# Mixers' output projections: weight units split four ahead of their tile, a list of banks per tile, more tiles begun early

## The reference, cut to what matters

```python
h = h + rmsnorm(mixed, gain)        # layers 1, 2; mixed = mixer(rmsnorm(h)) @ w_out
h = h + rmsnorm(swiglu_ffn(rmsnorm(h)), gain)
x = x + mixed                       # layers 3, 4: no norm behind the mixer
x = x + conv_ffn(rmsnorm(x))
```

## Time and profile before

| | |
|---|---|
| runs (device us) | 2430.51, 2433.38, 2432.56; median 2432.56 |
| the profiled execution | 2432.12 us, of which the span from the first to the last instruction is 2430.3 us |
| mean granted TensorE clock | 0.994 of full speed |
| busy: PE, PEld, DVE, ACT, POOL | 2376.9 (98%), 1941.5 (80%), 1322.0 (54%), 1020.6 (42%), 60.6 us (2%) |
| DMA | 214.12 MB, 88 GB/s over the span |

### The profile page before, as it was taken

How to read it: one execution, slowest core, us unless ns; L and a number is a source line. 1 busy time by engine, 2 the same in 40 slices (tenths; PEclk the granted TensorE clock), 3 DMA queues, 4 the chain that set the end, 5 groups by cost and what they waited for, 6 DMA issues and landing times.

```text
span 2430.3 us, 29906 instructions
## 1 busy us (share of the span) xinstructions
PE 2376.9 (98%) x11072; PEld 1941.5 (80%) x11072; DVE 1322.0 (54%) x1869; ACT 1020.6 (42%) x1630; POOL 60.6 (2%) x96
## 2 busy tenths in 40 slices
PE   8999999999999999999999989999999999999999
PEld 7777788888788877888887768788888877788887
DVE  5665644432537866444325665777533555677731
ACT  5555423222447854322324664444322544444420
POOL 1000000000002200000000000000001000000000
PEclk9999999999999999999999999999999999999999
DMA  4112222332221112223322113222323222222332
GB/s 147 61 60 71 87 95 87 104 119 89 78 96 61 53 55 87 93 95 102 120 90 80 61 36 112 78 95 95 121 95 102 78 70 70 95 96 95 105 107 82
DMA packets 68785, 214.12 MB, mean 88 GB/s; under 512 B 7056, under 2 KB 17808, under 8 KB 68688
## 3 DMA queue, kind: packets, MB, share of 16 engines
q1 hardware_dynamic: 67280, 210.72, 26.2%
q0 software_dynamic: 1408, 2.08, 0.3%
HBM read 210.67 MB, written 2.10 MB: 88 GB/s over the span
## 4 chain that ended last, share of the span: by engine, by line
PE 92%; DVE 4%; ACT 3%; issue 1%; DMA 0%; SPq 0%; ACTq 0%; DVEq 0%
PE bank L257 25%; PE bank L259 24%; PE bank L258 24%; PE bank L319 7%; PE bank L327 5%; PE bank L916 1%; PE bank L907 1%; PE bank L947 1%; PE bank L1290 1%; DVE w_lo L231 0%; ACT w_hi L226 0%; PE bank L1803 0%; PE bank L2221 0%; PE bank L2233 0%; PE bank L1335 0%
## 5 line engine op out<-in xcount | busy, mean ns | idle before, releaser
L257 PE MATMUL bank<-x_hi,w_hi 128*128 128x512 f32 x1792 | 708.6, 395 | 8.6 <-DVE w_lo L231 7.1
L259 PE MATMUL bank<-x_hi,w_lo 128*128 128x512 f32 x1792 | 699.4, 390 | 0.0
L258 PE MATMUL bank<-x_lo,w_hi 128*128 128x512 f32 x1792 | 699.1, 390 | 0.0
L231 DVE TENSOR_TENSOR w_lo<-raw,w_hi 128x1024 fp32r<-128x1024 f32 (+1 forms) x368 | 471.4, 1291 | 258.4 <-ACT w_hi L226 257.6
L226 ACT ACTIVATE w_hi<-raw 128x1024 fp32r<-128x1024 f32 (+1 forms) x368 | 404.1, 1108 | 115.9 <-PE bank L259 68.1
L257 PEld LDWEIGHTS bank<-x_hi,w_hi 128*128 128x128 f32 x1792 | 337.6, 188 | 83.9 <-issue 13.1
L259 PEld LDWEIGHTS bank<-x_hi,w_lo 128*128 128x128 f32 x1792 | 337.3, 188 | 71.5
L258 PEld LDWEIGHTS bank<-x_lo,w_hi 128*128 128x128 f32 x1792 | 337.8, 189 | 69.9 <-issue 1.9
L258 PE MATMUL bank<-up_a_lo,w_hi 128*128 128x512 f32 x704 | 273.9, 389 | 0.0
L257 PE MATMUL bank<-up_a_hi,w_hi 128*128 128x512 f32 x704 | 273.9, 389 | 0.0
L259 PE MATMUL bank<-up_a_hi,w_lo 128*128 128x512 f32 x704 | 273.9, 389 | 0.0
(11 more groups left out here) (355 smaller groups left out, 2675.1 us busy)
## 6 DMA issues: line engine op xcount, KB each, us to landing
raw<-in_w_up SPq DMA_DIRECT2D x176, 512.0 KB, 3.2
raw<-in_w_down SPq DMA_DIRECT2D x64, 704.0 KB, 4.2
raw<-in_w_fox_qk SPq DMA_DIRECT2D x16, 512.0 KB, 3.2
raw<-in_w_hgrn_qf SPq DMA_DIRECT2D x16, 512.0 KB, 3.2
raw<-in_w_fox_v SPq DMA_DIRECT2D x8, 512.0 KB, 4.0
raw<-in_w_fox_out SPq DMA_DIRECT2D x8, 512.0 KB, 3.2
raw<-in_w_hgrn_v SPq DMA_DIRECT2D x8, 512.0 KB, 3.4
raw<-in_w_hgrn_g SPq DMA_DIRECT2D x8, 512.0 KB, 3.2
```

What stands on the lines that cost most here:

```text
L231: nc.vector.tensor_tensor(w_lo[:, slot, 0:size], raw[:, slot % 2, 0:size], w_hi[:, slot, 0:size].bitcast(F32), ALU.subtract).then_inc(sem( ...
L257: nc.tensor.matmul(out, w[0], x[0], start=first, stop=False)
L258: nc.tensor.matmul(out, w[0], x[1], start=False, stop=False)
L259: return nc.tensor.matmul(out, w[1], x[0], start=False, stop=last)
```

## The change: what it does

- `act_out` and `dve_out` split four units ahead instead of two (`fourth_ahead`): at tile i ACT converts unit i+4 and then empties the tile; DVE does its share of tile i first and then splits unit i+4. Behind the last unit come the first three units of the next phase, at tiles 4 to 6.
- So units 2 and 3 must be split inside the mixer. Fox: `convert` and `split` take `fox_out` 2 and 3 in the last pair. Sb: `convert(10)` before and `convert(11)` behind the copies of `sb_fail_b`, and `split(10)`, `split(11)` before `output(3)` on DVE. Gla: unit 3 for p = 4, behind `mix_hi` on ACT and `mix_lo` on DVE. Hgrn had them already.
- Every mixer has a list with one bank for each of the 8 tiles, and `pe_out` waits for the last tile that had the same bank. Fox goes from two banks to four, gla from (0, 1, 3) to (0, 1, 3, 4, 0, 1, 3, 0); hgrn and sb keep theirs.
- Fox makes 6 blocks of tile 1 before `turn(m, 1)` instead of 3, and 7 blocks of tile 2 around `bring(m)`, with a new wait for the copies of `fox_pt_a`, which empty bank 2. Gla makes 6 blocks of tile 3 early.
- In gla, for p = 4 and 5, DVE norms the previous head before it makes the chunk states, not behind them.

```diff
-        def out_early(pe, name, c, ks, ready, banks=(0, 1)):
+        def out_early(pe, name, c, ks, ready, banks):
...
-            out_products(pe, name, c, u_of(name) + c, ks, ready, not done, False, banks[c % len(banks)])
+            out_products(pe, name, c, u_of(name) + c, ks, ready, not done, False, banks[c])
...
-                    if len(banks) > 2:
-                        if i >= len(banks):
-                            pe.wait_ge(sem("y_ready" if s < 4 else "h_ready"), DT * s + i - len(banks) + 1)
-                    elif (s, j, c) > (0, 0, 1):
-                        bank_free(pe, s, i)
+                    if banks[i] in banks[:i]:
+                        before = i - 1 - banks[:i][::-1].index(banks[i])
+                        pe.wait_ge(sem("y_ready" if s < 4 else "h_ready"), DT * s + before + 1)
...
-        def act_out(act, s, name, banks=(0, 1), split=0):
-            def body(j, u, last):
-                for c in range(4):
-                    if 4 * j + c >= split:
-                        ahead(convert_act, act, name, c, u + c, last)
-                    third_ahead(convert_act, act, name, c, last)
-                    tile_act(act, s, 4 * j + c, banks[(4 * j + c) % len(banks)], u + c)
-            unrolled(name, body)
...
+        def fourth_ahead(convert, eng, name, i):
+
+            e = i + 4
+            if e < DT:
+                convert(eng, e % 4, u_of(name) + e, IN_UNIT)
+            elif e < DT + 3 and name in following:
+                convert(eng, e % 4, following[name].first + e - DT, following[name].size)
+
+        def act_out(act, s, name, banks):
+            for i in range(DT):
+                fourth_ahead(convert_act, act, name, i)
+                tile_act(act, s, i, banks[i], u_of(name) + i)
+
+        def dve_out(dve, s, name, banks):
+            for i in range(DT):
+                tile_dve(dve, s, i, banks[i], u_of(name) + i)
+                fourth_ahead(convert_dve, dve, name, i)
...
+        FOX_OUT = (0, 1, 2, 3) * 2
...
-                out_early(pe, "fox_out", 0, list(range(7)), out_ready)
+                part(0, list(range(7)))
                 turn(m, 0)
-                out_early(pe, "fox_out", 1, list(range(3)), out_ready)
+                part(1, list(range(6)))
                 turn(m, 1)
-                out_early(pe, "fox_out", 1, [3, 4], out_ready)
+                part(1, [6])
+                wait(pe, "fx_pt", 6 * m + 3)
+                part(2, list(range(3)))
                 bring(m)
-                out_early(pe, "fox_out", 1, [5, 6], out_ready)
-            pe_out(pe, 0, "fox_out", out_ready)
+                part(2, list(range(3, 7)))
+            pe_out(pe, 0, "fox_out", out_ready, FOX_OUT)
...
-                elif i < 2 * FOX_PAIRS + 2:
+                elif i < 2 * FOX_PAIRS + 4:
                     convert_act(act, i % 4, u_of("fox_out") + i - 2 * FOX_PAIRS, IN_UNIT)
...
-        HGRN_OUT = (0, 1, 2, 3)
+        HGRN_OUT = (0, 1, 2, 3) * 2
...
+        SB_OUT = (0, 1) * 4
...
             turned(3, 0)
+            convert(10)
             turned(3, 1)
+            convert(11)
             output(3)
             exp_ln_table()
...
             pool_low(3)
+            split(10)
+            split(11)
             output(3)
...
-        GLA_OUT = (0, 1, 3)
+        GLA_OUT = (0, 1, 3, 4, 0, 1, 3, 0)
...
             part(2, [4, 5])
+            part(3, [0, 1, 2, 3, 4, 5])
             pe_out(pe, 6, "gla_out", out_ready, GLA_OUT)
...
+                if mix and not proj:
+                    ahead(convert_act, act, "gla_out", 1, u_out + 1, False)
...
+                if norm and not proj:
+                    normed()
                 if mix:
                     wait(dve, "gla_dec", m + 1)
...
+                if norm and proj:
+                    normed()
...
+                if mix and not proj:
+                    ahead(convert_dve, dve, "gla_out", 1, u_out + 1, False)
```

More of the change, by code:

```diff
@@ L771, in out_products, with pe_out @@
             return ins
-        def out_early(pe, name, c, ks, ready, banks=(0, 1)):
+        def out_early(pe, name, c, ks, ready, banks):
             done = early.setdefault((name, c), [])
-            out_products(pe, name, c, u_of(name) + c, ks, ready, not done, False, banks[c % len(banks)])
+            out_products(pe, name, c, u_of(name) + c, ks, ready, not done, False, banks[c])
             done += ks
-        def pe_out(pe, s, name, ready, banks=(0, 1)):
+        def pe_out(pe, s, name, ready, banks):
             def body(j, u, last):
@@ L789, in body @@
                     ks = [k for k in range(DT) if k not in done]
                     out_products(pe, name, c, u + c, ks, ready, not done, True,
-                                 banks[i % len(banks)]).then_inc(sem("unit_used"), 1)
-            bodies(pe, name, body)
+                                 banks[i]).then_inc(sem("unit_used"), 1)
+            unrolled(name, body)
             end_pe(pe, s)
-        def act_out(act, s, name, banks=(0, 1), split=0):
-            def body(j, u, last):
-                for c in range(4):
-                    if 4 * j + c >= split:
-                        ahead(convert_act, act, name, c, u + c, last)
-                    third_ahead(convert_act, act, name, c, last)
-                    tile_act(act, s, 4 * j + c, banks[(4 * j + c) % len(banks)], u + c)
-            unrolled(name, body)
@@ L939, in out_ready, with part @@
                 wait(e, "fx_out", k + 1)
+            def part(c, ks):
+                out_early(pe, "fox_out", c, ks, out_ready, FOX_OUT)
             def scores(m):
@@ L1056, in act_fox @@
             output(FOX_PAIRS - 1)
-            act_out(act, 0, "fox_out")
+            act_out(act, 0, "fox_out", FOX_OUT)
         def dve_fox(dve):
@@ L1177, in dve_fox @@
             output(FOX_PAIRS - 1)
-            dve_out(dve, 0, "fox_out")
+            dve_out(dve, 0, "fox_out", FOX_OUT)
         def pool_fox(pool):
@@ L1715, in dve_hgrn @@
                         take(m, 1)
-            dve_out(dve, 2, "hgrn_out", HGRN_OUT, 2)
+            dve_out(dve, 2, "hgrn_out", HGRN_OUT)
         def pool_hgrn(pool):
@@ L1874, in pe_sb @@
             wait(pe, "sb_px", 4)
-            out_early(pe, "sb_out", 0, [7, 6, 0], out_ready)
+            out_early(pe, "sb_out", 0, [7, 6, 0], out_ready, SB_OUT)
             turn(2, 1)
@@ L1884, in pe_sb @@
             pooled(3)
-            out_early(pe, "sb_out", 0, [1, 5], out_ready)
+            out_early(pe, "sb_out", 0, [1, 5], out_ready, SB_OUT)
             turn(3, 0)
             wait(pe, "sb_pscaled", 4)
-            out_early(pe, "sb_out", 1, [7, 6, 0], out_ready)
+            out_early(pe, "sb_out", 1, [7, 6, 0], out_ready, SB_OUT)
             turn(3, 1)
-            out_early(pe, "sb_out", 1, [1, 5, 2], out_ready)
+            out_early(pe, "sb_out", 1, [1, 5, 2], out_ready, SB_OUT)
             wait(pe, "sb_out", 3)
             values(3)
-            out_early(pe, "sb_out", 0, [2, 4], out_ready)
-            out_early(pe, "sb_out", 1, [4], out_ready)
-            pe_out(pe, 4, "sb_out", out_ready)
+            out_early(pe, "sb_out", 0, [2, 4], out_ready, SB_OUT)
+            out_early(pe, "sb_out", 1, [4], out_ready, SB_OUT)
+            pe_out(pe, 4, "sb_out", out_ready, SB_OUT)
         def act_sb(act):
@@ L2133, in dve_sb @@
             pool_low(3)
+            split(10)
+            split(11)
             output(3)
[L2135 removed]
+            dve_out(dve, 4, "sb_out", SB_OUT)
         def pool_sb(pool):
@@ L2372, in dve_gla, with normed @@
                     ahead(convert_dve, dve, "gla_out", 0, u_out, False)
+                def normed():
+                    for vt in range(2):
+                        wait(dve, "gla_back", 2 * o + vt + 1)
+                        wait(dve, "gla_out", 2 * (o - 1) + vt + 1)
+                        g = COL["gla_norm"] + vt
+                        nc.vector.scalar_tensor_tensor(B[2 + vt], ps[g_tokens[vt]][:], cols[:, g:g + 1], ggate[:, 2 * o + vt, :],
+                                                       ALU.mult, ALU.mult).then_inc(sem("gla_on"), 1)
+                if norm and not proj:
+                    normed()
                 if mix:
@@ L2385, in dve_gla @@
                                                            ALU.add).then_inc(sem("gla_st"), 1)
[L2386 to L2390, removed]
-                        nc.vector.scalar_tensor_tensor(B[2 + vt], ps[g_tokens[vt]][:], cols[:, g:g + 1], ggate[:, 2 * o + vt, :],
-                                                       ALU.mult, ALU.mult).then_inc(sem("gla_on"), 1)
+                if norm and proj:
+                    normed()
                 if proj:
```

10 lines of the change are left out of this document (5 added, 5 removed).

## The result

| | before | after |
|---|---|---|
| median, us | 2432.85 (2430.51 to 2433.38, 4 runs) | 2418.89 (2414.60 to 2420.43, 4 runs) |
| profiled execution, us | 2432.12, span 2430.3 | 2420.23, span 2418.4 |
| mean granted clock | 0.994 | 0.994 |

The ratio after / before is 0.9942, 95% interval 0.9924 to 0.9959: 14.0 us faster, where 9.4 were forecast and the range ended at 2419.5. So the direction was right, and the size lay 0.6 us outside the range. In two later comparisons, on two chips and with nothing edited, the two kernels stand 10.6 and 9.6 us apart. The traces of the changed kernel give 10.1 us to the stages that hold the projections. Much of what follows is about the other 4 us. The profiled execution of the kernel before is not one of its four runs.

What follows compares the result with a forecast made beforehand. TensorE, busy 98% of the span, was taken as the bound, so only its waits or slow clock could be won: 2.0 + 2.1 + 1.0 + 1.2 + 3.1 = 9.4 us, from 2432.56 to 2423.2, range 2419.5 to 2427.5.

Steps and rivals of the forecast that it cites:

- Fox, 2.0: Fox's end: waits before the second turn (0.84), tile 2 (0.74) and around `bring(7)` (0.4) go, 2.0 us gained.
- Hgrn, 2.1 and 1.0 for the clock: Hgrn's tile 4: wait falls from 2.70 to 0.55 us; the slow clock behind it, worth 0 to 1.4, taken as 1.0.
- Sb, 1.2: Sb's tile 2: with unit 2 split earlier, DVE empties bank 0 sooner; start at 1452.1 instead of 1453.30.
- Gla, 3.1: Gla: 1.4 us from the norm before the states, 1.7 from tile 3's wait for unit 3's split; bounds 1.7 to 3.45.
- the 18 matmuls of tile 3: Gla: early blocks of tile 3, 4.1 us, standing in front of the last blocks, as part of why the second wait goes.
- B: Waits move along their chains in fox or gla, and hgrn's clock fall comes elsewhere: gain 4.2, 2428.4 us; chance 0.11.
- C: Slower: five conversions inside mixers wait for DMAs and hold copies PE needs, 3.2 us each: 2439 us; chance 0.03.
- D: Slower by clock: every bank change in fox and gla lets it fall, ten tiles cost 14 us: 2438; chance 0.02.

Runs made afterwards that it cites:

- the old blocks: Changed kernel with fox's early blocks as before, four banks and early conversions kept: 2417.08 us, one execution; fox 184.79 us, 1.28 longer.
- the old walk: Changed kernel with hgrn's unit 4 converted and split at tile 2 again, not tile 0: 2425.18 us median, against 2419.97 beside it.
- The run with extra products: Changed kernel plus 14 unread products behind the means at the end of fox, hgrn and the first two FFNs: 2415.64 us, 0.9936 of the kernel before.

## Why the prediction was wrong, point by point

- **Fox, 2.0:** 2.03. The split into 1.25 for the early blocks and 0.75 for the banks holds (the old blocks cost 1.28). Conversions in front of the copies cost nothing in the changed kernel.
- **Hgrn, 2.1 and 1.0 for the clock:** the wait went from 2.70 to 0.64 (0.55 forecast), 2.06. The split, not the bank, was what ended last, shown by the old walk. The clock was mis-sized: 1.6 in place of 1.0. The prediction counted seven slow matmuls, 1.4 us, and took off for executions in which the clock does not fall. The stretch costs 1.6 (3.66 of the stage less 2.06 of the wait), since the matmuls at its two ends are slow in part; and the clock fell behind this wait in all three traces that have it (both of the kernel before, and the old walk). This is 0.6 of the 0.7 us by which the sum is short.
- **Sb, 1.2:** 1.24, the wait 0.26.
- **Gla, 3.1:** 3.16. 1.32 from the norm's move, the rest from unit 3; the 18 matmuls of tile 3 that the prediction set in front were not needed.
- **Rivals B, C, D:** B's first half did not come, no wait took another's place. Its second half did in small, in the stages behind the projections: 1.0 us more behind gla, 1.0 less behind sb, and 0.9 to 1.0 more behind fox in two of the three traces. C: none of the five conversions now inside the mixers waited for a DMA. Six in the walks did, for 0.2 to 1.6 us (those that start at 230.11 and 233.37 in fox, 901.19 and 904.41 in hgrn, 2029.08 and 2031.48 in gla), and PE waited for none of them. D: no clock fell inside a projection. The Trainium skill ("TensorE: Matmul & The Clock Gate", section "A second HAM failure mode: psum-queue depth-cycling") tells of a kernel whose clock swung because TensorE idled briefly between its groups of matmuls while it went through PSUM banks. The trace after shows neither the idling nor the swing: 33.5 us busy of 33.5 and 1.00 over gla's tiles.
- **The step that failed** is the one behind the sum: "From the median: 2432.56 - 9.4 = 2423.2", with a range for which "the runs differ by 2.9" was the whole of the scatter. The 40 later executions of the kernel before spread over 6.5 us (2428.05 to 2434.51), the 14 of the changed one over 6.9 (2414.60 to 2421.46). The mechanism held, and the sum itself is only 0.7 short (9.4 against 10.1). The base was 2.1 us over the level of 40 later executions, and the four executions of the changed kernel 1.2 under the level of its 14. 10.4 + 2.4 (four runs of before, 2432.85 against 2430.46) + 1.2 = 14.0. So both groups of four lay to the far side of their levels, and nothing in the change accounts for it. Pure luck is a thin account too: four executions drawn at random from each of the later groups (40 and 10) lie 13.9 us or more apart in about 1 of 90 draws. The cause of those 4 us stays open.
- **A reading that was too short:** "2430.3 - 2376.9 = 53 us in all" is the time in which TensorE stands still. Matmuls at the lower clock count as busy, so the 30.7 us at 0.50 in the trace before, half of them lost, are for the most part on top of it. The run with extra products took 5.2 us from there.
- **What differed between executions** is the start and the clock, in code that no edit touched. In the start, PE's first matmul comes at 8.59 and 7.84, when the first tile of the input has landed and ACT has made `x_hi` of it. Then 12 and 5 steps from one matmul to the next are 0.43 us long, and one more lies in between (0.37 and 0.28), before the pace is full: 0.75 + 1.5 = 2.25 us, the whole difference of the start column. The rows are PE's of the kernel before, then of the changed one, and the change of pace in it:

```profile
8.59 0.77 PE L319 MATMUL bank<-w_hi,x_hi 128*128 128x512 f32 x1 [8.59 <-ACT x_hi L403]
9.15 0.63 PE L319 MATMUL bank<-w_lo,x_hi 128*128 128x512 f32 x1
```

```profile
7.84 0.77 PE L319 MATMUL bank<-w_hi,x_hi 128*128 128x512 f32 x1 [7.84 <-ACT x_hi L403]
...
10.11 0.63 PE L319 MATMUL bank<-w_lo,x_hi 128*128 128x512 f32 x1
10.54 0.45 PE L319 MATMUL bank<-w_hi,x_hi 128*128 128x512 f32 x1
10.82 0.39 PE L319 MATMUL bank<-w_lo,x_hi 128*128 128x512 f32 x1
```

At the full clock they start 0.227 apart. (The granted clock is not recorded so early in the trace; the pace shows it.) Over all 14 traces, all with the same code up to there, the start lies between 70.38 and 73.17.
- **Open:** why the four executions of the kernel before in the first comparison stood 2.4 us over the level of the later ones. Their clocks are not on record, nor is the chip of that comparison; the profiled execution beside them has 0.994 and a late start, 72.92. Two of the four (2433.38, 2433.14) lie where later only executions at 0.992 lie. The two later chips give the kernel before the same median to 0.2 us. And why taking hgrn's edit back cost 1.5 us more than its stage shows: the median clock of its ten executions is 0.993, that of the five beside them 0.994, so it is likely the clock elsewhere, but not shown.

## What to carry to other kernels

When TensorE is busy 98% of the time, list its waits with their true length (pitch, not drawn end), and for each ask which of its conditions ends last; four such chains gave 8.5 us of waits and 1.6 of clock, 10.1 in all, where 9.4 were summed. Price the clock too: matmuls at the lower one look busy. A bracket names one releaser: look at when that one ended, as with `y` and the split in hgrn. For a change of some 0.4%, don't hang the forecast on the median of three executions: compare stages between the same two waits, which repeat to 0.06 us where the clock does the same in both, and put the start and the clock into the range by themselves.

## What the runs showed of the hardware that was not expected

- Behind one and the same wait of 4.01 us, at fox's end, the clock stayed at 1.00 in 3 of 12 traces, fell for 3.4 us in 4, and for 6.8 us in 5. The stage behind it (ffn1) then took 365.8 to 365.9, 367.2 to 367.3 and 368.1 to 368.5 us: the same wait cost 0, 1.4 or 2.2 to 2.7 us more. Behind sb's wait of 3.14 us it fell in 2 of 12 traces, behind hgrn's of 2.70 in 3 of 3. Length alone doesn't decide it.
- Executions of one kernel come in groups by clock: 40 executions of one kernel fall into 32 at a mean clock of 0.994 and 8 at 0.992, 3.7 us apart in the median.
- Matmuls whose results nobody reads, in waits of TensorE, made the kernel 5.2 us faster. They did not keep the clock up everywhere: in both traces that have them it fell behind a wait of 2.2 us in hgrn, at 753 and 752, where none of the other twelve shows it, and in one for 6.8 us at 1425, at sb's wait of 3.14.
